# Gate products of a recurrent unit, from whole 128-row products to alternating products of the lower and the upper 64 rows

## The chip, the cores and the metric

The kernel runs on one core of a Trainium2 chip. The metric is the device time of one execution in microseconds (us); lower is better. The engines are TensorE (PE, its weight loads PEld), VectorE (DVE), ScalarE (ACT), GpSimd (POOL) and SyncE (SP), which issues most DMAs.

## What is computed

Two blocks run one after the other on a sequence of 1024 tokens of width 1024. The second block holds a real-gated linear recurrent unit, which is where the change lies. Its gates are products within 16 groups of 64 channels, cut from the reference:

```python
def rg_lru(u, w_rg, b_rg, w_ig, b_ig, lru_lambda):
    ub = uf.reshape(B, S, LRU_BLOCKS, LRU_BLOCK_DIM)          # 16 groups of 64 channels
    r = jax.nn.sigmoid(jnp.einsum('bshi,hij->bshj', ub, w_rg).reshape(B, S, LRU_WIDTH) + b_rg)
    i = jax.nn.sigmoid(jnp.einsum('bshi,hij->bshj', ub, w_ig).reshape(B, S, LRU_WIDTH) + b_ig)
    log_a = -LRU_C * r * jax.nn.softplus(-lru_lambda)
    a = jnp.exp(log_a)
    xin = jnp.sqrt(-jnp.expm1(2.0 * log_a)) * (i * uf)
    # h_t = a_t * h_{t-1} + xin_t, an associative scan over the sequence
```

Ahead of it, u = h @ w_in (a part of it) goes through a causal convolution of 4 taps; behind it, h is multiplied by silu(g_lru) and goes into a product with w_pb.

## The kernel before

All of it is one program with one instruction stream per engine; the order of each stream is written out by hand, and semaphores tie the streams together. Features lie on the 128 partitions, tokens along the free dimension, so a tile c of the recurrent unit holds 128 channels, two groups of 64. PSUM has eight banks of 512 float32 words per partition. The class `Banks` gives the fills (one output of 512 words each) to the banks in turn: fill n takes bank n % 8 and waits (`wait_free`) until fill n - 8 has been drained by the engine that `list_fills_2` names for it.

The weight stream comes in tiles of 128x1024 words. SP loads a tile (`load_tile`) when the last product with the tile before it in its slot is done; POOL then splits it into a high part (L913, a cast) and a low part (L916, a subtraction), and TensorE forms each float32 product in three passes of these parts (`three_passes`, L1017 to L1019). A fill of 8 contraction tiles is 24 such products.

The recurrent unit is worked on in rounds. Round q of 0 to 3 handles c = 2q and 2q+1, and round 4 ends it:

- TensorE fills ("lu", c, h) for both c and both halves h of the tokens (4 fills), then, from round 1 on, ("lg", c-2, h) (4 fills), and then the gate products ("lr", c, h) and ("li", c, h) (8 fills of one float32 product each, L1536, which stands in the trace as two instructions). These use `rgig`, loaded once, as plain float32. Before each c it waits for `uc_ready`, the convolution of that c.
- VectorE (`convolve`) copies a "lu" bank (L2859) and forms the four taps (L2862, L2864, L2866, L2869) for both c. Then `output(c - 2)` multiplies yl by th (L2875) for both c of the round before. Then it forms i*u (L2887) when ("li", c, 1) is drained, and with what ScalarE gives it L2889, L2890, L2893 and the scan L2894. Behind the last round, L2899 forms `yl_lo` from `yl` and `yl_hi`.
- ScalarE drains the "lg" banks with Silu (L2041) and the gate banks with Sigmoid (L2050 into `ra`, L2052 into `ii`). Ahead of a Sigmoid of "lr" it waits, from round 1 on, for `yl_ready`, which counts the outputs: that of tile c - 2. Then Tanh and Exp (L2057, L2058), Sqrt (L2061), with a table load where the function's table changes. Behind the last round, L2065 forms `yl_hi`.

Behind round 4's "lg" fills TensorE fills ("GB", 0, h) and ("GB", 1, h), and then ("B", 0, h), which needs all eight tiles of `yl_lo` (`yl_split`). More GB and B fills and the last product with w_o end the kernel.

Elsewhere, in the first block's state-space mixer, L1203 already forms float32 products of 64 rows and 128 columns, in turn on the lower and the upper 64 partitions and into two banks, with four products of all 128 rows (L1198) between groups of 16 such instructions; only the last of each group's products signals.

In the layout, `rgig` holds for each c a 128x128 matrix for each of the two gates, with the 64x64 weights of the tile's two groups on its diagonal and zeros elsewhere.

Of the kernel before, what the change touches and what calls it, by code (L numbers as in the profile page):

```python
# [9 lines left out]
ACT = mybir.ActivationFunctionType  # L10
AX_X = mybir.AxisListType.X

P = 128
# [4 lines left out]
HALF = 512  # L18
# [317 lines left out]
def build_program(nc, a, out):  # L336
    with ExitStack() as ctx:
# [27 lines left out]
        def at(offset, *dims):  # L365
            placed[0] += 1
            return place(f"buffer{placed[0]}", offset, dims, F32)
# [5 lines left out]
        K = 1024  # L373
# [62 lines left out]
        def col(name, j):  # L436
            return cols[:, COLS[name][0] + j:COLS[name][0] + j + 1]
# [127 lines left out]
        att = at(4 * K, HEADS, SEQ)  # L565
        merged2 = at(32 * K, KD, SEQ)
        mt2 = at(48 * K, 4, HALF)
        rgig = at(48 * K, 8, 2, P)
        uc = at(4 * K, 2, SEQ)
        ra = at(6 * K, 2, SEQ)  # L570
        th = at(12 * K, 2, SEQ)
        ii = at(14 * K, 2, SEQ)
# [43 lines left out]
        drained2 = {"act": sem("act_drained2"), "dve": sem("dve_drained2")}  # L616
# [34 lines left out]
        rgig_loaded = sem("rgig_loaded")  # L651
# [61 lines left out]
        def _(sp):  # L713
# [164 lines left out]
                load_tile(i)  # L878

            sp.wait_ge(merged2_ready, 16)  # L880
            sp.dma_start(rgig.rearrange("p a b c -> p (a b c)"), a["rgig"]).then_inc(rgig_loaded, 16)
            for i in range(I_LRU + 4, I_WO2):
                load_tile(i)
            b2.wait_full(sp, ("GB", 7, 1))
# [119 lines left out]
        def _(pe):  # L1004
            mm, turn = nc.tensor.matmul, nc.tensor.transpose
# [509 lines left out]
            for q in range(5):  # L1515
                if q < 4:
                    for c in (2 * q, 2 * q + 1):
                        w = wait_split_tile(pe, n_tile)
                        n_tile += 1
                        for h in range(2):  # L1520
                            split_feature_tile(b2, ("lu", c, h), w, hT_parts, h, KD)
                if q > 0:
                    for c in (2 * q - 2, 2 * q - 1):
                        w = wait_split_tile(pe, n_tile)
                        n_tile += 1
                        for h in range(2):
                            split_feature_tile(b2, ("lg", c, h), w, hT_parts, h, KD)
                if q == 0:
                    pe.wait_ge(rgig_loaded, 16)
                if q < 4:  # L1530
                    for c in (2 * q, 2 * q + 1):
                        pe.wait_ge(uc_ready, c + 1)
                        for h in range(2):
                            for name, j in (("lr", 0), ("li", 1)):
                                bank = b2.wait_free(pe, (name, c, h))
                                mm(bank[:], rgig[:, c, j, :], uc[:, c % 2, h * HALF:(h + 1) * HALF],  # L1536
                                   start=True, stop=True).then_inc(full2, 1)

            for i, (name, f) in enumerate(B2_TILES):
# [31 lines left out]
        def _(act):  # L1571
# [464 lines left out]
            for q in range(5):  # L2036
                if q > 0:
                    for c in (2 * q - 2, 2 * q - 1):
                        for h in range(2):
                            bank = b2.wait_full(act, ("lg", c, h))  # L2040
                            fn(yl[:, c, h * HALF:(h + 1) * HALF], bank[:], ACT.Silu).then_inc(drained2["act"], 1)  # L2041
                if q == 4:
                    break
                for c in (2 * q, 2 * q + 1):
                    for h in range(2):
                        hs = slice(h * HALF, (h + 1) * HALF)
                        bank = b2.wait_full(act, ("lr", c, h))
                        if q:
                            act.wait_ge(yl_ready, c - 1)
                        fn(ra[:, c % 2, hs], bank[:], ACT.Sigmoid, bias=col("b_rg", c)).then_inc(drained2["act"], 1)  # L2050
                        bank = b2.wait_full(act, ("li", c, h))
                        fn(ii[:, c % 2, hs], bank[:], ACT.Sigmoid, bias=col("b_ig", c)).then_inc(drained2["act"], 1)  # L2052
                for c in (2 * q, 2 * q + 1):
                    b2.wait_drained(act, ("li", c, 1))
                    if c == 0:
                        act.wait_ge(lru_s_ready, 2)
                    fn(th[:, c % 2, :], ra[:, c % 2, :], ACT.Tanh, scale=lru_ns[:, c:c + 1])  # L2057
                    fn(ra[:, c % 2, :], ra[:, c % 2, :], ACT.Exp, scale=lru_s[:, c:c + 1]).then_inc(act_to_lru, 1)  # L2058
                for c in (2 * q, 2 * q + 1):
                    act.wait_ge(lru_to_act, c + 1)  # L2060
                    fn(th[:, c % 2, :], th[:, c % 2, :], ACT.Sqrt).then_inc(act_to_lru, 1)  # L2061
# [876 lines left out]
def _layouts(inputs):  # L2938
# [3 lines left out]
    c = {}  # L2942
# [68 lines left out]
    c["bsB"] = np.ascontiguousarray(bs.transpose(1, 2, 0, 3).reshape(128, 512))  # L3011
    c["wglu"] = np.ascontiguousarray(f["s5_w_glu"][0].reshape(2, 128, 256).transpose(1, 0, 2).reshape(128, 512))
    c["wr"] = np.ascontiguousarray(f["w_router"][0].reshape(8, 128, 16).transpose(1, 0, 2).reshape(128, 128))
    rg = np.zeros((128, 8, 2, 128), np.float32)
    for j, w in enumerate((f["w_rg_2"][0], f["w_ig_2"][0])):
        for i in range(16):
            s = 64 * (i % 2)
            rg[s:s + 64, i // 2, j, s:s + 64] = w[i]
    c["rgig"] = rg.reshape(128, 2048)
    for k in ("w_gate", "w_up", "w_down"):  # L3020
        c[k] = np.ascontiguousarray(f[k][0])
    return c
# [15 lines left out]
```

## Time and profile before

| | |
|---|---|
| median of 3 runs | 2842.61 us (2842.43 to 2844.53) |
| span of the profiled execution | 2842.6 us |
| TensorE products, busy | 2794.4 us, 98% |
| TensorE weight loads, busy | 2291.8 us, 81% |
| VectorE, busy | 1724.6 us, 61% |
| ScalarE, busy | 1308.0 us, 46% |
| GpSimd, busy | 735.0 us, 26% |

The times are of whole executions; the span is from the first to the last instruction of one execution that was profiled, and no other time is given for that execution. A busy time is the union of an engine's instructions; TensorE's products overlap each other in it, since a product is in the pipeline longer than the next one waits to start. The recurrent unit's rounds lie between about 2372 and 2576 us of the span.

### The profile page before, as it was taken

How to read it: one execution, taken by the hardware profiler on the slowest of the kernel's cores; microseconds unless marked ns; L12 is line 12 of the kernel's file. 1: busy time of each engine (PE TensorE's matmuls, PEld its weight loads, DVE VectorE, ACT ScalarE, POOL GpSimd, SP SyncE). 2: the span in 40 equal slices, each digit the busy share in tenths (PEclk: the TensorE clock that was granted, in tenths of full speed). 3: DMA queues.
4: the chain of work that ended last, by engine and by line, in shares of the span. 5: the costliest groups of instructions: out<-in, count | busy, mean ns of one | idle time of the engine just before them, and what ended most of it. 6: DMA issues, size and time to landing. Idle time of an engine off the chain costs nothing.

```text
span 2842.6 us, 34799 instructions
## 1 busy us (share of the span) xinstructions
PE 2794.4 (98%) x13206; PEld 2291.8 (81%) x13206; DVE 1724.6 (61%) x1880; ACT 1308.0 (46%) x1542; POOL 735.0 (26%) x284
## 2 busy tenths in 40 slices
PE   7999999999999999999999999999999999999999
PEld 6887888478888888888888877888988887778887
DVE  8962114888888888888888884131312614864133
ACT  5131013477777777777777763130312312242021
POOL 0012231002222233333332222313222223433330
PEclk9999999999999999999999999999999999999999
DMA  5021114699999999999999953111111411111131
GB/s 165 30 68 37 38 62 155 246 395 388 383 382 383 383 383 383 381 383 381 383 382 381 377 229 112 52 50 55 49 56 56 139 45 67 42 41 45 52 126 59
DMA packets 127074, 555.96 MB, mean 196 GB/s; under 512 B 14545, under 2 KB 22753, under 8 KB 93825
## 3 DMA queue, kind: packets, MB, share of 16 engines
q1 hardware_dynamic: 116160, 523.91, 48.6%
q0 software_dynamic: 5328, 20.07, 2.5%
q10 hardware_dynamic: 5490, 10.62, 1.0%
q8 instruction: 70, 1.15, 0.2%
q14 instruction: 26, 0.21, 0.0%
HBM read 521.42 MB, written 32.09 MB: 195 GB/s over the span
## 4 chain that ended last, share of the span: by engine, by line
PE 90%; DVE 7%; ACT 2%; issue 1%; DMA 0%; ACTq 0%; POOL 0%; SPq 0%; DVEq 0%
PE bank L1351 23%; PE bank L1017 19%; PE bank L1019 19%; PE bank L1018 19%; PE bank L1364 2%; PE bank L1484 1%; PE bank L1455 1%; PE bank L1536 1%; PE bank L1477 1%; ACT buffer L1973 1%; PE bank L1414 0%; PE bank L1373 0%; DVE heT_lo L2628 0%; DVE buffer L2306 0%; ACT heT_hi L1896 0%
## 5 line engine op out<-in xcount | busy, mean ns | idle before, releaser
L2578 DVE TENSOR_TENSOR slots_lo<-buffer,slots_hi 128x2048 fp32r<-128x2048 f32 x383 | 849.2, 2284 | 103.9 <-ACT slots_hi L1850 103.9
L1850 ACT ACTIVATE slots_hi<-buffer 128x2048 fp32r<-128x2048 f32 x384 | 709.1, 1950 | 44.3 <-PE bank L1351 27.5
L1017 PE MATMUL bank<-hT_hi,ring_hi 128*128 128x512 f32 x1216 | 483.9, 398 | 5.2 <-DVE hT_lo L2694 2.2
L1019 PE MATMUL bank<-hT_hi,ring_lo 128*128 128x512 f32 x1216 | 474.0, 390 | 0.0
L1018 PE MATMUL bank<-hT_lo,ring_hi 128*128 128x512 f32 x1216 | 473.6, 389 | 0.0
L976 POOL DMA_INDIRECT xacc<-buffer x15 | 276.6, 18439 | 619.9 <-ACT buffer L1918 619.9
L913 POOL CAST ring_hi<-buffer 128x1024 fp32r<-128x1024 f32 x101 | 114.7, 1136 | 835.9 <-DMA buffer<-in_wstream 806.6
L916 POOL TENSOR_TENSOR ring_lo<-buffer,ring_hi 128x1024 fp32r<-128x1024 f32 x111 | 285.2, 2572 | 51.2 <-ACT ring_hi L1584 43.1
L1017 PEld LDWEIGHTS bank<-hT_hi,ring_hi 128*128 128x128 f32 x1216 | 228.4, 188 | 57.2 <-DVE hT_lo L2694 7.1
L1019 PEld LDWEIGHTS bank<-hT_hi,ring_lo 128*128 128x128 f32 x1216 | 228.2, 188 | 48.2
L1018 PEld LDWEIGHTS bank<-hT_lo,ring_hi 128*128 128x128 f32 x1216 | 228.5, 188 | 46.4 <-issue 1.2
L1351 PE MATMUL bank<-slots_hi,xsT_hi 128*128 128x512 f32 x960 | 257.8, 390 | 4.0 <-DVE xsT_lo L2596 4.0
L1351 PE MATMUL bank<-slots_lo,xsT_hi 128*128 128x512 f32 x960 | 257.4, 390 | 0.0
L1351 PE MATMUL bank<-slots_hi,xsT_lo 128*128 128x512 f32 x960 | 257.4, 390 | 0.0
L1351 PEld LDWEIGHTS bank<-slots_hi,xsT_hi 128*128 128x128 f32 x960 | 180.9, 189 | 41.8 <-issue 4.2
L1351 PEld LDWEIGHTS bank<-slots_lo,xsT_hi 128*128 128x128 f32 x960 | 180.8, 188 | 37.7
L1351 PEld LDWEIGHTS bank<-slots_hi,xsT_lo 128*128 128x128 f32 x960 | 180.8, 188 | 37.7
L1017 PE MATMUL bank<-slots_hi,heT_hi 128*128 128x512 f32 x512 | 202.5, 395 | 3.1 <-DVE heT_lo L2628 3.1
L1019 PE MATMUL bank<-slots_hi,heT_lo 128*128 128x512 f32 x512 | 199.5, 390 | 0.0
L1018 PE MATMUL bank<-slots_lo,heT_hi 128*128 128x512 f32 x512 | 199.4, 389 | 0.0
L1017 PEld LDWEIGHTS bank<-slots_hi,heT_hi 128*128 128x128 f32 x512 | 96.0, 188 | 29.6 <-issue 6.5
L1019 PEld LDWEIGHTS bank<-slots_hi,heT_lo 128*128 128x128 f32 x512 | 96.1, 188 | 20.5
(508 smaller groups left out, 3957.0 us busy)
## 6 DMA issues: line engine op xcount, KB each, us to landing
buffer<-in_w_gate SPq DMA_DIRECT2D x128, 1024.0 KB, 7.6
buffer<-in_w_up SPq DMA_DIRECT2D x128, 1024.0 KB, 4.9
buffer<-in_w_down SPq DMA_DIRECT2D x128, 1024.0 KB, 8.1
buffer<-in_wstream SPq DMA_DIRECT2D x154, 512.0 KB, 3.5
buffer<-in_x SPq DMA_DIRECT2D x16, 512.0 KB, 8.4
od<-buffer ACTq DMA_DIRECT2D x24, 260.0 KB, 2.1
xacc<-buffer SPq DMA_DIRECT2D x8, 512.0 KB, 2.8
h2d<-buffer SPq DMA_DIRECT2D x8, 512.0 KB, 4.9
```

Source lines behind the costliest of these rows:

```text
L913: nc.gpsimd.tensor_copy(high_tile(i), raw).then_inc(tile_high_ready, 1)
L916: nc.gpsimd.tensor_tensor(low_tile(i), raw, high_tile(i).bitcast(F32), ALU.subtract).then_inc(tile_split, 1)
L976: nc.gpsimd.indirect_dma_start(out=xacc, out_offset=bass.IndirectOffsetOnAxis(ap=idx_scatter, axis=0), in_=ys, in_offset=None, compute_op= ...
L1017: mm(bank, lhs[0], rhs[0], start=first, stop=False)
L1018: mm(bank, lhs[0], rhs[1], start=False, stop=False)
L1019: return mm(bank, lhs[1], rhs[0], start=False, stop=last)
L1351: last = mm(psum[first_bank + c][:], x[:, k, :], w_[:, c * HALF:(c + 1) * HALF], start=(k == 0 and x is xsT_hi and w_ is w[0]), stop=(k == ...
L1364: last = mm(psum[4 + c][:], x[:, KD - 1, :], w_[:, c * HALF:(c + 1) * HALF], start=False, stop=x is xsT_lo)
L1455: last = mm(bank[:, i, :], Qh[:, h, tt * P:(tt + 1) * P], Kh[g][:, h, (tt - nw + 1) * P:(tt + 1) * P], start=True, stop=True)
L1477: last = turn(bank[:, h * P:(h + 1) * P], SM[tt % 2][:, h, (nw - 1 - w_) * P:(nw - w_) * P], ident)
L1850: fn(slots_hi[:, n_ % NH, :], slots[n_ % NS], ACT.Copy).then_inc(slot_high_ready, 1)
L2578: tt2(slots_lo[:, place_of(n_), :], slots[n_ % NS], slots_hi[:, n_ % NH, :].bitcast(F32), ALU.subtract).then_inc(slot_split, 1)
```

## The change

`rgig` holds half as much: for each c, rows 0 to 63 are the weights of the lower group, r gate and i gate side by side (64 + 64 columns), and rows 64 to 127 those of the upper group, i gate and r gate. Each gate product now contracts 64 rows: "lr" those of partitions 0 to 63, "li" those of 64 to 127. A bank so holds both gates of one group: in "lr" the lower half of the partitions is r and the upper half is i, both of the lower group; in "li" the lower half is i and the upper half is r, both of the upper group. ScalarE therefore drains each bank with two Sigmoids of 64x512, the second of which marks it as drained, and two of the four for each c and h read one half of the partitions and write the other.

```diff
--- before.py
+++ after.py
@@ -565,7 +565,7 @@
         att = at(4 * K, HEADS, SEQ)
         merged2 = at(32 * K, KD, SEQ)
         mt2 = at(48 * K, 4, HALF)
-        rgig = at(48 * K, 8, 2, P)
+        rgig = at(48 * K, 8, P)
         uc = at(4 * K, 2, SEQ)
         ra = at(6 * K, 2, SEQ)
         th = at(12 * K, 2, SEQ)
@@ -878,7 +878,7 @@
                 load_tile(i)
 
             sp.wait_ge(merged2_ready, 16)
-            sp.dma_start(rgig.rearrange("p a b c -> p (a b c)"), a["rgig"]).then_inc(rgig_loaded, 16)
+            sp.dma_start(rgig.rearrange("p a b -> p (a b)"), a["rgig"]).then_inc(rgig_loaded, 16)
             for i in range(I_LRU + 4, I_WO2):
                 load_tile(i)
             b2.wait_full(sp, ("GB", 7, 1))
@@ -1531,9 +1531,9 @@
                     for c in (2 * q, 2 * q + 1):
                         pe.wait_ge(uc_ready, c + 1)
                         for h in range(2):
-                            for name, j in (("lr", 0), ("li", 1)):
+                            for name, s in (("lr", 0), ("li", 64)):
                                 bank = b2.wait_free(pe, (name, c, h))
-                                mm(bank[:], rgig[:, c, j, :], uc[:, c % 2, h * HALF:(h + 1) * HALF],
+                                mm(bank[:], rgig[s:s + 64, c, :], uc[s:s + 64, c % 2, h * HALF:(h + 1) * HALF],
                                    start=True, stop=True).then_inc(full2, 1)
 
             for i, (name, f) in enumerate(B2_TILES):
@@ -2047,9 +2047,14 @@
                         bank = b2.wait_full(act, ("lr", c, h))
                         if q:
                             act.wait_ge(yl_ready, c - 1)
-                        fn(ra[:, c % 2, hs], bank[:], ACT.Sigmoid, bias=col("b_rg", c)).then_inc(drained2["act"], 1)
+                        low, high = slice(0, 64), slice(64, P)
+                        fn(ra[low, c % 2, hs], bank[low, :], ACT.Sigmoid, bias=col("b_rg", c)[low])
+                        fn(ii[low, c % 2, hs], bank[high, :], ACT.Sigmoid, bias=col("b_ig", c)[low]).then_inc(
+                            drained2["act"], 1)
                         bank = b2.wait_full(act, ("li", c, h))
-                        fn(ii[:, c % 2, hs], bank[:], ACT.Sigmoid, bias=col("b_ig", c)).then_inc(drained2["act"], 1)
+                        fn(ii[high, c % 2, hs], bank[low, :], ACT.Sigmoid, bias=col("b_ig", c)[high])
+                        fn(ra[high, c % 2, hs], bank[high, :], ACT.Sigmoid, bias=col("b_rg", c)[high]).then_inc(
+                            drained2["act"], 1)
                 for c in (2 * q, 2 * q + 1):
                     b2.wait_drained(act, ("li", c, 1))
                     if c == 0:
@@ -3011,12 +3016,9 @@
     c["bsB"] = np.ascontiguousarray(bs.transpose(1, 2, 0, 3).reshape(128, 512))
     c["wglu"] = np.ascontiguousarray(f["s5_w_glu"][0].reshape(2, 128, 256).transpose(1, 0, 2).reshape(128, 512))
     c["wr"] = np.ascontiguousarray(f["w_router"][0].reshape(8, 128, 16).transpose(1, 0, 2).reshape(128, 128))
-    rg = np.zeros((128, 8, 2, 128), np.float32)
-    for j, w in enumerate((f["w_rg_2"][0], f["w_ig_2"][0])):
-        for i in range(16):
-            s = 64 * (i % 2)
-            rg[s:s + 64, i // 2, j, s:s + 64] = w[i]
-    c["rgig"] = rg.reshape(128, 2048)
+    pairs = np.concatenate([f["w_rg_2"][0], f["w_ig_2"][0]], axis=2).reshape(8, 2, 64, 128)
+    pairs[:, 1] = np.concatenate([f["w_ig_2"][0], f["w_rg_2"][0]], axis=2).reshape(8, 2, 64, 128)[:, 1]
+    c["rgig"] = np.ascontiguousarray(pairs.transpose(1, 2, 0, 3).reshape(128, 1024))
     for k in ("w_gate", "w_up", "w_down"):
         c[k] = np.ascontiguousarray(f[k][0])
     return c
```

## Rows read from the trace of the kernel before

**Rows 1.** The page: busy time, share of the span and instructions of each engine.
```profile
PE 2794.4 (98%) x13206; PEld 2291.8 (81%) x13206; DVE 1724.6 (61%) x1880; ACT 1308.0 (46%) x1542; POOL 735.0 (26%) x284
```

**Rows 2.** Chain that ended last, 2300 to 2640: start us, us, what.
```profile
2398.47 3.70 PE bank L1536 x8
...
2445.71 6.87 PE bank L1536 x16
...
2546.51 6.87 PE bank L1536 x16
2553.38 0.23 PE bank L1017
```

**Rows 3.** Waits of PE, 2394 to the end: us in total, times, longest.
```profile
PE bank L1536 <- DVE buffer L2869: 0.4, 1, 0.4
```

**Rows 4.** Timeline of PE, 186 to 200.5: start us, us, instruction.
```profile
187.91 0.71 PE L1198 MATMUL bank<-buffer 128*128 128x128 f32 x4
188.56 1.16 PE L1203 MATMUL bank<-buffer 64*128 64x128 f32 x16
189.65 0.71 PE L1198 MATMUL bank<-buffer 128*128 128x128 f32 x4
```

**Rows 5.** Timeline of ACT, 2385 to 2510 (round 1).
```profile
2447.66 0.69 ACT L2050 ACTIVATE buffer<-bank,buffer 128x512 f32<-128x512 f32 x1
...
2449.38 0.70 ACT L2052 ACTIVATE buffer<-bank,buffer 128x512 f32<-128x512 f32 x1
...
2453.20 1.14 ACT L2057 ACTIVATE buffer<-buffer 128x1024 f32<-128x1024 f32 x1
```

**Rows 6.** Groups of ACT by form: busy us, mean ns | idle before.
```profile
L2041 ACT ACTIVATE buffer<-bank 128x512 f32<-128x512 f32 x16 | 9.5, 598 | 94.0 <-PE bank L1019 94.0
...
L1693 ACT ACTIVATE buffer<-bank 16x512 f32<-16x512 f32 x4 | 2.1, 574 | 1.0 <-PE bank L1166 1.0
```

**Rows 7.** Timeline of DVE, 2385 to 2510.
```profile
2490.55 3.31 DVE L2875 TENSOR_TENSOR buffer<-buffer 128x1024 f32<-128x1024 f32 x1
```

**Rows 8.** Single lines of DVE, 2402 to 2560: minimum/median/maximum ns, first and last start.
```profile
L2862 DVE TENSOR_SCALAR buffer<-buffer x12: 547/548/1589, 2421.3 to 2537.4; 128x512 f32<-128x512 f32 x12
L2864 DVE SCALAR_TENSOR_TENSOR buffer<-buffer x24: 750/752/1527, 2422.9 to 2538.7; 128x512 f32<-128x512 f32 x24
L2869 DVE SCALAR_TENSOR_TENSOR buffer<-buffer x6: 1408/2088/2773, 2429.1 to 2539.5; 128x512 f32<-128x512 f32 x6
L2875 DVE TENSOR_TENSOR buffer<-buffer x6: 1225/2263/3305, 2440.3 to 2547.2; 128x1024 f32<-128x1024 f32 x6
L2894 DVE TENSOR_TENSOR_SCAN buffer<-buffer x6: 2291/2650/3008, 2413.8 to 2518.2; 128x1024 f32<-128x1024 f32 x6
```

**Rows 9.** Timeline of POOL, 2385 to 2600: one tile.
```profile
2477.75 1.08 POOL L913 CAST ring_hi<-buffer 128x1024 fp32r<-128x1024 f32 x1 [4.76 <-DMA buffer<-in_wstream]
2478.91 2.72 POOL L916 TENSOR_TENSOR ring_lo<-buffer,ring_hi 128x1024 fp32r<-128x1024 f32 x1
```

**Rows 10.** Timeline of all engines, 2392 to 2402 (round 0).
```profile
2394.51 3.59 PE L1536 MATMUL bank<-buffer 128*128 128x512 f32 x8
...
2395.57 0.69 ACT L2050 ACTIVATE buffer<-bank,buffer 128x512 f32<-128x512 f32 x1 [49.22 <-PE bank L1536]
```

**Rows 11.** Timelines of ACT and DVE from 2540, and the line of yl_lo.
```profile
2554.00 1.14 ACT L2057 ACTIVATE buffer<-buffer 128x1024 f32<-128x1024 f32 x1
...
2575.82 1.23 DVE L2875 TENSOR_TENSOR buffer<-buffer 128x1024 f32<-128x1024 f32 x1 [0.94 <-ACT buffer L2041]
2578.17 12.23 DVE L2899 TENSOR_TENSOR yl_lo<-buffer,yl_hi 128x1024 fp32r<-128x1024 f32 x8 [1.13 <-ACT yl_hi L2065]
...
L1018 PE MATMUL bank<-yl_lo,ring_hi x18: 389/389/389, 2597.0 to 2619.4; 128*128 128x512 f32 x18
```

**Rows 12.** The page: DMA issues, KB each, us to landing.
```profile
buffer<-in_wstream SPq DMA_DIRECT2D x154, 512.0 KB, 3.5
```

**Rows 13.** Waits of PE; busy by stretch (PE, PEld, DVE, ACT, POOL), clock, DMA.
```profile
PE bank L1351 <- DVE xsT_lo L2596: 4.0, 1, 4.0
...
578.00:584.00 6.00, 6.00 (x18) 4.76 (x17) 4.79 (x6) 4.52 (x4) 0.54 (x1) 0.60 0.92 355
```

## The prediction

> **What bounds the kernel now.** The page comes first: TensorE is busy 98% of the span, and the chain that ended last runs through it here, so what shortens TensorE's own work shortens the kernel, as long as nothing else is late [rows 1]. Next, the chain in order of time in the stretch that the diff touches. I count from the first gate product (2394.51 us = 0 [rows 10]) and call "gates" the products of L1536 of one round q: they start at 0, 51.2, 101.6 and 152.0; the later ones take 6.87 us for 16 instructions (each of the 8 products of a round is two), 0.429 each, and the last round's end at 158.87 (2553.38) [rows 2]. So a round is 50.4 us on TensorE: 6.87 of gates and 43.5 of "lu" and "lg" products. TensorE waits for nothing from here to the end but 0.4 us in round 0 [rows 3]: the stretch is TensorE's, and the reader should ask how close behind the other two engines are. The answer is in the timelines of ScalarE and VectorE [rows 5, 7].
>
> **TensorE's part.** Each gate product was 128x128 by 128x512, half of its weights zeros; now it is 64x128 by 64x512, in the same number. A 64-row product alone is no shorter: it streams the same 512 columns. The gain can only come from a "lr" product (rows 0 to 63) and a "li" product (rows 64 to 127) running at once. The trace has this pattern at L1203: 16 such instructions, two and two on alternate row halves, 128 columns wide, take 1.09 us (188.56 to 189.65) [rows 4]. A quarter of the columns is a quarter of 0.429, 0.107 each, so 16 in a row would take 1.72; 1.09 is half of that and 0.23 more. The four full ones ahead, between two such groups, take 0.65 instead of 4 x 0.107 = 0.43 [rows 4], 0.22 for the change of form. For one round: 6.87/2 = 3.43, +0.23, +0.22, +0.16 because the half without a partner is four times as long here: 4.0 us. That is 2.87 less per round in rounds 1 to 3. In round 0 the second half waits for the convolution of c=1: its products started at 3.96 after a 0.36 wait [rows 2, 3], and VectorE isn't earlier; they now end at 3.96+2.3 = 6.2 instead of 51.2-43.5 = 7.7, 1.4 less. Were TensorE all that mattered, the sum would be 3 x 2.87 + 1.4 = 10.0 us.
>
> **ScalarE's part.** Four Sigmoids of 128x512 for each c become eight of 64x512, 16 for a round instead of 8. Back to back they start every 0.573 us (the first at 2447.66, the fourth at 2449.38) [rows 5]. No half-height one is in the trace; the nearest are 16x512 from a bank, 574 ns, against 598 for 128x512 [rows 6], so I give half the height the full price (bounds: half of it, 0.29, if height did count, which these two rows exclude, and 0.69, its own duration, if they don't overlap). A round's Sigmoids take 16 x 0.573 = 9.17 instead of 5.54 (2447.66 to 2453.20, the last ones at TensorE's pace [rows 5]): Tanh and all behind it come 3.6 us later after the first Sigmoid.
>
> **Who waits for that.** First Sigmoid of round q, then L2057 and the Exp, Sqrt and scans, then the convolutions of round q+1, then output(2q) at L2875, and for that the first Sigmoid of q+1 waits (on yl_ready, L2050): a loop through ScalarE and VectorE. From L2057 to the end of output is 2493.86-2453.20 = 40.7 [rows 5, 7] (the end is 2490.55+3.31). Before, the loop was 5.54+40.7 = 46.2 in a round of 50.4; now it is 9.17+40.7+0.05 = **49.9**, while TensorE's round would be 4.0+43.5 = 47.5. The loop becomes the longer one. It holds TensorE by the banks: the first "lu" (or, at the end, "lg") product behind the gates takes the bank of ("lr",2q,0), eight fills back, which is free after two Sigmoids, 0.573+0.69 = 1.27 after the first.
>
> The 40.7 holds waits of VectorE for GpSimd, which prepares three weight tiles in it. In each round one instruction of each of these kinds is stretched, the longest against the shortest of its kind: L2862 1.59 against 0.55, L2864 1.53 against 0.75, L2875 3.31 against 1.23, L2894 3.01 against 2.29, and both L2869, 2.77 and 1.41, where the same form at L2864 takes 0.75 [rows 8]: 1.0+0.8+2.1+0.7+2.0+0.7 = 7.3. The loop is 42.6 with none. L2869's 2.77 lies at 2479.4, beside L916's 2.72 from 2478.91 [rows 9]; a tile holds VectorE up for at most about 1.05 (L913) and 2.4 (L916 without its own waiting), 3.45, and three tiles paid in full make 53.0. The Trainium skill ("SBUF — State Buffer", Who interferes with whom) has it that of two such operations the second to issue fully blocks until the first finishes. The stretches agree; by this rule with nothing harmless between, the sum would go by the 53.0. After the change the tiles come about 2.9 us earlier and VectorE's work 3.6 later, so the first tile falls among L2889 to L2894, ops with no free gap between, and the last leaves L2875 for the convolution. I take 0.6 more than now: **50.5**.
>
> **The sum.** Round 1's gates start at 51.2-1.4 = 49.8, first Sigmoid 1.95 later as now (2447.66 against 2445.71, a table load lies between [rows 2, 5]): 51.75; the loop from round 0 (first Sigmoid 1.06 [rows 10], +9.17+40.7 = 50.9) isn't late yet. Round 2: gates at 97.3, but the first Sigmoid at 51.75+50.5 = 102.25 instead of 99.25, and TensorE goes on at 103.5, not 101.3, a wait of 2.2. Round 3: gates at 147.0, first Sigmoid 152.75, "lg" from 154.0 after a wait of 3.0; before 158.87. Then B(0) needs all of yl_lo. From the first Sigmoid of round 3: 9.17, then 23.05 from L2057 (2554.00) to the end of the last output (2577.05), then 13.35 until L2899 is done (2590.40) [rows 11]: 152.75+45.6 = 198.3. TensorE comes there 43.6 after 154.0, at 197.6; before, it came at 202.5 (2597.0) [rows 11]. Everything behind hangs on TensorE and moves with it: 202.5-198.3 = **4.2 us** less. The smaller DMA of rgig, and the bias and weight layouts, cost nothing: the load, now 512 KB, lies behind "lu" products, and TensorE doesn't wait for it even at 1024 KB [rows 3]; not covered, it would be one landing of such a size, 3.5 us, once [rows 12]. The profiled span is 2842.6, the median 2842.61, so the sum is made against the same number: 2838.4.
>
> **Rivals.**
> *TensorE stays the bound* (the loop under 48.0): all 10.0 us come, 2832.6. For it: the loop without stretches is 42.6. Against: three tiles a round will still be prepared, and at the measured stretches it is 49.9. The Trainium skill ("TensorEngine Tiling (Array Packing)", Theoretical Speedup) gives up to 2x for a contraction of 64 rows; by that alone half of the some 27.4 us of gates, 13.7, would come, 2828.9. The rows of L1203 show 1.72/1.09 = 1.6x, edges included [rows 4].
> *No overlap*: the increments on every second instruction or the bank waits between them, which L1203 does not have, keep the halves apart. Then 6.87 stays, the edges add 0.4 a round, the loop (50.5) hides under 50.8: 2844.2.
> *The clock*: TensorE's new waits of 2 to 3 us. After an idle 3.97 us the granted clock was 0.60 (partly the lower level, 1.2 GHz) over the next 6 us, 18 products instead of 26, some 2 to 3 us lost [rows 13]. Round 2's loss is covered by the loop; round 3's isn't: TensorE reaches B(0) at 200.6, 2840.7.
> *Slower*: a half-height Sigmoid whose input and output lie 64 partitions apart costs more. Each 0.01 us is paid 16 times in three loops and the tail, 0.64 us. At 0.65 each the gain is gone; at 0.74 the kernel is 0.2% slower; at 0.80 it is 9 to 10 us slower, 2852. Against: the price doesn't show in 16x512 [rows 6].
>
> **How the numbers follow.** The forecast (loop binds, 48 to 52 long) 0.62, with 0.22 of it at 49.7 or less, where it gives over 5.7 us; TensorE bound 0.11; no overlap 0.13; clock 0.08; slower 0.06. A measurement can tell about 0.2%, 5.7 us. Faster 0.22+0.11 = 0.33; same 0.40+0.13+0.08 = 0.61; slower 0.06. Likeliest time 2838.4. The range reaches from nearly all of TensorE's gain (2832.6) past no overlap (2844.2), 2833.0 to 2844.8. The loop with all three tiles in full gives 54.1+2 x 53.0+45.6 = 205.7, 3.2 more than 202.5, 2845.8; that all of them fall so is not likely, and it stays outside.
>
> **What will show it.** 16 gate instructions in about 4 us; half-height Sigmoids every 0.573; the first Sigmoid of rounds 2 and 3 some 50.5 after the one before, released by L2875 and not by TensorE; TensorE waiting 2 to 3 us behind the gates of rounds 2 and 3 for a Sigmoid; little or no wait at B(0). Gates of 6.9 us prove me wrong about the overlap; rounds of 47.5 without waits, about the loop.

## The result, and the profile after

| | before | changed |
|---|---|---|
| median | 2843.34 us (4 runs) | 2858.4 us (2856.79 to 2861.96, 4 runs) |
| ratio to before | | 1.0052, 95% interval 1.0040 to 1.0064 |
| span of the profiled execution | 2842.6 | 2857.3 |

The change makes the kernel 15 us slower. The prediction said 4.2 us faster, with a range up to 2844.8. The profile after, in the order of the prediction. (In the changed kernel ScalarE's Sigmoids are L2051, L2052, L2055 and L2056; lines of VectorE's part are 5 further on: L2892 is i*u, L2894 and L2895 follow, L2899 is the scan, L2869 and L2874 are taps, L2880 is the output, L2904 forms yl_lo.)

TensorE's part, from its timeline (start us, us, instruction), beside [rows 2, 10]; the last row is the first product of B(0):

```profile
2392.77 1.99 PE L1536 MATMUL bank<-buffer 64*128 64x512 f32 x8
...
2500.97 3.79 PE L1536 MATMUL bank<-buffer 64*128 64x512 f32 x8 [4.43 <-DVE buffer L2874]
...
2561.56 0.77 PE L1017 MATMUL bank<-hT_hi,ring_hi 128*128 128x512 f32 x1 [0.32 <-ACT buffer L2052]
...
2609.67 0.47 PE L1017 MATMUL bank<-yl_hi,ring_hi 128*128 128x512 f32 x1 [3.55 <-issue]
```

Eight gate instructions take 1.99 us with the pipeline's end, where eight took 3.59 in [rows 10]: the two row halves do run at once. But TensorE now waits: 4.43 us in rounds 2 and 3 for the second convolution, and 3.55 us ahead of B(0). The profile names no releaser there ("issue"); the kernel has TensorE wait for all of yl_lo ahead of B(0) (`yl_split`), and L2904, which forms it, ends at 2609.56. Its waits in the stretch (us in total, times, longest) were 0.4 in all in [rows 3]:

```profile
PE bank L1536 <- DVE buffer L2874: 11.0, 4, 4.4
PE bank L1017 <- issue: 3.5, 1, 3.5
PE bank L1017 <- ACT buffer L2052: 2.7, 3, 2.1
PE bank L1536 <- DVE buffer L2864: 2.1, 2, 1.1
```

ScalarE, the first Sigmoid of round 1 and then round 2, beside [rows 5]:

```profile
2447.13 0.68 ACT L2051 ACTIVATE buffer<-bank,buffer 64x512 f32<-64x512 f32 x1
...
2502.25 1.28 ACT L2051 ACT_TABLE_LOAD   x1 [9.15 <-DVE buffer L2880]
2503.54 0.68 ACT L2051 ACTIVATE buffer<-bank,buffer 64x512 f32<-64x512 f32 x1
2504.24 0.69 ACT L2052 ACTIVATE buffer<-bank,buffer 64x512 f32<-64x512 f32 x1
2504.95 0.68 ACT L2055 ACTIVATE buffer<-bank,buffer 64x512 f32<-64x512 f32 x1
...
2514.78 1.15 ACT L2062 ACTIVATE buffer<-buffer 128x1024 f32<-128x1024 f32 x1
```

Three things stand here. The round's first Sigmoid comes 56.4 us after that of round 1 (2447.13 to 2503.54), released by the output (L2880): the loop sets the pace, as forecast, but it is 56.4 long and not 50.5. The Sigmoids start every 0.70 us, 16 in 11.24 (2503.54 to 2514.78), not every 0.573. And the table load stands behind the wait for the output, 1.3 us inside the loop.

VectorE and GpSimd in the same turn of the loop (timelines), beside [rows 8, 9]. Each cast shown begins a weight tile, and its subtraction (L916, shown for the first tile) follows it:

```profile
2463.34 1.95 DVE L2895 SCALAR_TENSOR_TENSOR buffer<-buffer 128x1024 f32<-128x1024 f32 x1
2465.20 3.43 DVE L2892 TENSOR_TENSOR buffer<-buffer 128x1024 f32<-128x1024 f32 x1
...
2474.65 1.88 DVE L2898 TENSOR_TENSOR buffer<-buffer 128x1024 f32<-128x1024 f32 x1
2476.57 4.37 DVE L2899 TENSOR_TENSOR_SCAN buffer<-buffer 128x1024 f32<-128x1024 f32 x1
...
2486.29 3.55 DVE L2869 SCALAR_TENSOR_TENSOR buffer<-buffer 128x512 f32<-128x512 f32 x2
...
2495.97 4.15 DVE L2869 SCALAR_TENSOR_TENSOR buffer<-buffer 128x512 f32<-128x512 f32 x2
```

```profile
2463.05 1.16 POOL L913 CAST ring_hi<-buffer 128x1024 fp32r<-128x1024 f32 x1 [12.80 <-DMA buffer<-in_wstream]
2464.28 3.27 POOL L916 TENSOR_TENSOR ring_lo<-buffer,ring_hi 128x1024 fp32r<-128x1024 f32 x1
...
2474.04 1.41 POOL L913 CAST ring_hi<-buffer 128x1024 fp32r<-128x1024 f32 x1 [6.49 <-DMA buffer<-in_wstream]
...
2484.85 1.04 POOL L913 CAST ring_hi<-buffer 128x1024 fp32r<-128x1024 f32 x1 [6.07 <-DMA buffer<-in_wstream]
...
2495.77 1.06 POOL L913 CAST ring_hi<-buffer 128x1024 fp32r<-128x1024 f32 x1 [7.27 <-DMA buffer<-in_wstream]
```

Four tiles meet VectorE's dense work now, not three. By "stretch" I mean the time of an instruction beyond what it takes undisturbed. Against 1.23, 1.22, 1.22, 2.29 and twice 2 x 0.77 (the last two rows are two instructions each), the stretches are 0.7+2.2+0.7+2.1+2.0+2.6 = 10.3, against 7.3 before.

The loop adds up: 42.6 without stretches, +10.3, +2.07 for 16 Sigmoids at 0.70, +1.3 for the table load = 56.3; measured 56.4. Here 42.6 is the prediction's loop without stretches.

The start of B(0) in the kernel before, for comparison:

```profile
2596.75 0.39 PE L1017 MATMUL bank<-yl_hi,ring_hi 128*128 128x512 f32 x1
```

And the clock (from:to in us, the stretch's length, TensorE's busy time and products in it, granted clock, DMA share, GB/s; the last row is an earlier stretch, round 3):

```profile
2606.00:2612.00 6.00, 2.45 (x9) 0.92 0.26 89
2612.00:2618.00 6.00, 6.00 (x23) 0.80 0.00 0
2618.00:2624.00 6.00, 6.00 (x28) 1.00 0.09 23
2556.00:2562.00 6.00, 4.22 (x9) 0.50 0.00 0
```

After the wait of 3.55 us TensorE runs in part at the lower of its levels (1.2 of 2.4 GHz): 23 products in 6 us, where the next 6 us at full clock have 28. B(0) starts 12.9 us later than before (2609.67 against 2596.75), and the kernel's end comes 14.7 later. Of the 1.8 us between, 1.7 are lost in B(0)'s first 18 products, which take 5.78 us instead of 4.08 (2609.67 to 2615.45, before 2596.75 to 2600.83); behind them the two executions keep the same pace. The row of round 3 has a clock of 0.50 around its 4.43 us wait, and the eight gate instructions behind such a wait take 3.79 us instead of 1.99.

### The profile page after: what moved, and what is told of

The parts are those of the page before. It is cut to its first block, busy times and chain, and to the rows that moved or that the text cites. A ratio compares the mean times of both kernels' runs of the same rounds, so it can differ in the third digit from the quotient of the medians.

```text
span 2857.3 us, 34831 instructions
## 1 busy us (share of the span) xinstructions
PE 2789.8 (98%) x13206; PEld 2287.4 (80%) x13206; DVE 1733.5 (61%) x1880; ACT 1330.6 (47%) x1574; POOL 732.8 (26%) x284
## 4 chain that ended last, share of the span: by engine, by line
PE 84%; DVE 10%; ACT 3%; issue 1%; DMA 1%; POOL 0%; ACTq 0%; SPq 0%; DVEq 0%
PE bank L1351 23%; PE bank L1017 18%; PE bank L1019 18%; PE bank L1018 18%; PE bank L1364 2%; PE bank L1484 1%; DVE buffer L2869 1%; PE bank L1455 1%; DVE buffer L2899 1%; PE bank L1477 1%; ACT buffer L1973 1%; PE bank L1414 0%; PE bank L1373 0%; DVE heT_lo L2633 0%; DVE buffer L2898 0%
## 5 line engine op out<-in xcount | busy, mean ns | idle before, releaser
L913 POOL CAST ring_hi<-buffer 128x1024 fp32r<-128x1024 f32 x101 | 114.2, 1130 | 854.2 <-DMA buffer<-in_wstream 854.2
L916 POOL TENSOR_TENSOR ring_lo<-buffer,ring_hi 128x1024 fp32r<-128x1024 f32 x111 | 281.4, 2538 | 51.2 <-ACT ring_hi L1584 43.1
L1677 ACT ACTIVATE buffer<-bank,buffer 128x512 f32<-128x512 f32 x32 | 22.1, 690 | 195.2 <-PE bank L1019 195.2
```

The costliest lines, as they stand in the source:

```text
L913: nc.gpsimd.tensor_copy(high_tile(i), raw).then_inc(tile_high_ready, 1)
L916: nc.gpsimd.tensor_tensor(low_tile(i), raw, high_tile(i).bitcast(F32), ALU.subtract).then_inc(tile_split, 1)
```

## The experiments

All ratios are to the kernel before, run on the same chip (its medians there 2844.2 to 2844.5). The changed kernel itself (2858.4) ran beside a median of 2843.3, so a difference between runs of different groups can be off by about 1 us. First the four that take the change apart.

**The products alone.** The 64-row products of the change, with the drains of before:

```diff
-                        fn(ra[low, c % 2, hs], bank[low, :], ACT.Sigmoid, bias=col("b_rg", c)[low])
-                        fn(ii[low, c % 2, hs], bank[high, :], ACT.Sigmoid, bias=col("b_ig", c)[low]).then_inc(...)
+                        fn(ra[:, c % 2, hs], bank[:], ACT.Sigmoid, bias=col("b_rg", c)).then_inc(...)
... (the same for the "li" bank)
```

> Only the products of the change: 64-row gate products as in the changed kernel, but each bank drained by one Sigmoid of 128x512 as before, so that one half of ra and of ii holds the other gate (the output is not the reference's). Theory A (the loss is the loop through ScalarE and VectorE, not TensorE): the loop is 8 x 0.573 = 4.6 us of Sigmoids, a table load of 1.3 behind the wait if the output is late, and 41 to 44 from L2057 to the end of output, 47 to 49.9 in all against TensorE's 47.5; the kernel gains 4 to 10 us against the one before, about 2836. Rival B (the halves don't pay on TensorE, or its waits and the lower clock cost the time): gates of 4 us but lasting waits, no gain, or slower than before by 5 or more.

Measured: 2833.97 us, ratio 0.9964 (0.9950 to 0.9978), 10.5 us faster. TensorE in this run, from the chain that ended last (start us, us, instructions):

```profile
2399.71 1.99 PE bank L1536 x8
2445.44 3.63 PE bank L1536 x16
2492.86 3.63 PE bank L1536 x16
```

and, from the list of its waits over the stretch, the one (us in total, times, longest):

```profile
PE bank L1536 <- DVE buffer L2869: 1.9, 1, 1.9
```

The rounds are 47.42 us (2445.44 to 2492.86) with no wait behind round 0. TensorE's share of the change is worth what the prediction's sum gave it, 10.0 us, and the loss is not there. Its Sigmoids of full height start every 0.57 us.

**ScalarE's part alone.** The products of before, each bank drained by two half-height Sigmoids, nothing crossing:

```diff
-                        fn(ra[:, c % 2, hs], bank[:], ACT.Sigmoid, bias=col("b_rg", c)).then_inc(...)
+                        fn(ra[low, c % 2, hs], bank[low, :], ACT.Sigmoid, bias=col("b_rg", c)[low])
+                        fn(ra[high, c % 2, hs], bank[high, :], ACT.Sigmoid, bias=col("b_rg", c)[high]).then_inc(...)
... (the same for the "li" bank and `ii`)
```

> Only ScalarE's part of the change: the products of before (128 rows), each bank drained by two Sigmoids of 64x512, lower half to lower half and upper to upper, nothing crosses; the output is the reference's. If the 0.70 us from start to start comes from the half height or from changing halves: 0.70 here too, the loop 11.2+1.3+41 to 44 = 53.5 to 56.5, longer than TensorE's 50.4, so 8 to 17 us slower than before. If it comes from the crossing of partitions: 0.573, the loop 49.9, hidden, within 2 us of before.

Measured: 2859.8 us, 1.0057 (1.0040 to 1.0074); the Sigmoids start 0.70 us apart, and the table load waits for the output here too:

```profile
2504.58 1.28 ACT L2051 ACT_TABLE_LOAD   x1 [8.09 <-DVE buffer L2880]
```

The whole loss comes with ScalarE's part. With it, the faster products give nothing back (2859.8 with the old ones, 2858.4 with the new): the loop hides them.

**Is it the crossing?** The changed kernel with every Sigmoid writing the partitions that it reads (bank low to `ra[low]`, bank high to `ra[high]`, and so for `ii`):

> The changed kernel, but with every half-height Sigmoid writing the partitions that it reads (the gates land in the wrong tiles, the output is not the reference's). If crossing costs the 0.13 us: spacing 0.573, loop 2.1 shorter, about 6 us faster than the changed kernel. If not: 0.70 and 2858, as the changed kernel.

Measured: 2858.91, 1.0054 (1.0037 to 1.0071), spacing 0.70 (2501.36 to 2502.05 to 2502.76). Crossing costs nothing that shows.

This run shows one thing more. Its profiled execution was the fastest of its four, 2853.91 us, and its loop was 52.5 us long in rounds 1 and 2 (the first of these two turns starts at 2448.88):

```profile
2501.36 0.68 ACT L2051 ACTIVATE buffer<-bank,buffer 64x512 f32<-64x512 f32 x1
...
2553.89 0.68 ACT L2051 ACTIVATE buffer<-bank,buffer 64x512 f32<-64x512 f32 x1
```

The Sigmoids and the table load in it take what they take in the changed kernel. VectorE's stretches in a turn add up to 6.3 to 6.4 us instead of 10.3: the weight tiles fall at other places of its chain. So GpSimd's part of the loop is no fixed price; it depends on where the tiles fall.

**Where the wait stands.** The output is waited for because Tanh overwrites `th`; `ra` and `ii` are free earlier, since the gate products themselves come behind the convolution, and that behind the scans.

```diff
                         bank = b2.wait_full(act, ("lr", c, h))
-                        if q:
-                            act.wait_ge(yl_ready, c - 1)
...
+                    if q:
+                        act.wait_ge(yl_ready, c - 1)
                     fn(th[:, c % 2, :], ra[:, c % 2, :], ACT.Tanh, scale=lru_ns[:, c:c + 1])
```

> The changed kernel with the wait for the output of tile c-2 moved from the first Sigmoid to Tanh, the first to overwrite th. Theory A: the table load comes early again (1.3 less) and the first eight Sigmoids (5.6) and the output (1.3 to 2.5) leave the loop, which then runs by the second convolution, the gates and eight Sigmoids: 2.2+5.6+42.6 = about 50.4 instead of 56.5, near TensorE's round of before, 2840 to 2845. If the loop isn't what sets the time, it stays at 2858.

Measured: 2846.94, 1.0008 (0.9998 to 1.0018), 11.5 us less than the changed kernel (a little above what was expected, 2840 to 2845). This cuts the loop where the prediction says that it closes, so the loop is shown as the cause. TensorE's waits left in its profile, one of 4.65 us on the second convolution in round 2 and one at B(0):

```profile
PE bank L1536 <- DVE buffer L2874: 6.8, 3, 4.6
PE bank L1017 <- issue: 4.3, 1, 4.3
```

**The same on the kernel before**, as a control:

> The kernel before with the wait moved to Tanh and nothing else. Its loop (46.2) was hidden under TensorE's 50.4, so theory A expects no change, 2843 to 2845; a gain would mean that the wait cost something in the kernel before too.

Measured: 2843.82, 0.9998 (0.9988 to 1.0007). The wait cost nothing while TensorE set the pace.

**The table load.** The changed kernel, with a Sigmoid of one column ahead of the wait:

```diff
+                        if q and c == 2 * q and h == 0:
+                            fn(root[:, 0:1], root[:, 0:1], ACT.Sigmoid)
                         bank = b2.wait_full(act, ("lr", c, h))
```

> The changed kernel with a Sigmoid of one column ahead of the wait for the output, so that the table is loaded while ScalarE waits. Theory A: 1.3 us minus the 0.2 of the small Sigmoid, hidden too, leave the loop in rounds 1 to 3, in all 3 to 4 us against the changed kernel, 2854 to 2855.5. Rival (the load is hidden elsewhere): no change, 2858.

Measured: 2854.74, 1.0039 (1.0023 to 1.0054), 3.7 us below the changed kernel, as expected, though the two intervals overlap. The profile shows the mechanism: the load ends 7.9 us before the Sigmoid that needs it (2494.69 against 2502.55).

```profile
2493.41 1.28 ACT L2048 ACT_TABLE_LOAD   x1
2494.70 0.20 ACT L2048 ACTIVATE buffer<-buffer 128x1 f32<-128x1 f32 x1
2502.55 0.68 ACT L2053 ACTIVATE buffer<-bank,buffer 64x512 f32<-64x512 f32 x1 [7.64 <-DVE buffer L2882]
```

**Why 0.70 and not 0.573?** Three orders. First, with the wait at Tanh, the four Sigmoids that read the lower half of a bank, then the four that read the upper (the halves written alternate):

```diff
+                        fn(ra[low, c % 2, hs], bank[low, :], ACT.Sigmoid, bias=col("b_rg", c)[low])
+                        fn(ii[high, c % 2, hs], bank[low, :], ACT.Sigmoid, bias=col("b_ig", c)[high])
...
+                        fn(ii[low, c % 2, hs], b2.bank(("lr", c, h))[high, :], ACT.Sigmoid, bias=col("b_ig", c)[low]).then_inc(...)
+                        fn(ra[high, c % 2, hs], b2.bank(("li", c, h))[high, :], ACT.Sigmoid, bias=col("b_rg", c)[high]).then_inc(...)
```

> The kernel with the wait at Tanh (2846.9), with the Sigmoids of a tile c in another order: the four that read the lower half of a bank first, then the four that read the upper half; the output is the reference's. If the 0.70 us come from changing the half that is read from one Sigmoid to the next, six of eight now start after 0.57 and the loop is about 1 us shorter in each round, 2844 to 2846. If they come from the half height itself or the operands, the spacing stays 0.70 and the time too, or rises a little, since the first bank is free two Sigmoids later.

The spacing stayed at 0.69 to 0.71. The time was 2843.86, 0.9998 (0.9989 to 1.0008), 3 us below the run with the wait at Tanh, which the spacing doesn't explain. The intervals overlap, and the cause stays open; its profile has waits of 4.1 us in all on the second convolution and 2.3 at B(0), against 6.8 and 4.3 there. By this run alone I would have blamed half height. Second, the kernel before with half-height Sigmoids, grouped so that four in a row read and write the lower partitions, then four the upper:

> The kernel before with half-height Sigmoids (nothing crosses), for each tile c first the four on the lower 64 partitions, input, output and bias all there, then the four on the upper; the output is the reference's. If a Sigmoid waits for the one before it only where the half changes, six of eight start after 0.57; if half height itself forbids the overlap, all stay at 0.69 to 0.70.

```profile
2450.27 0.68 ACT L2051 ACTIVATE buffer<-bank,buffer 64x512 f32<-64x512 f32 x1
2450.86 0.67 ACT L2053 ACTIVATE buffer<-bank,buffer 64x512 f32<-64x512 f32 x1
2451.43 0.67 ACT L2051 ACTIVATE buffer<-bank,buffer 64x512 f32<-64x512 f32 x1
2452.00 0.68 ACT L2053 ACTIVATE buffer<-bank,buffer 64x512 f32<-64x512 f32 x1
2452.68 0.68 ACT L2056 ACTIVATE buffer<-bank,buffer 64x512 f32<-64x512 f32 x1
2453.27 0.67 ACT L2058 ACTIVATE buffer<-bank,buffer 64x512 f32<-64x512 f32 x1
```

Starts 0.57 apart while the half stays the same, 0.68 where it changes (2452.00 to 2452.68). So half height costs no more than full height. Two successive ones overlap by about 0.1 us if both use the same partitions, and not at all if the next changes the half. A change of the half that is read is enough (in the changed kernel 2503.54 to 2504.24: bank low, then bank high, both writing low), and so is a change of the half that is written, with that of its bias, which changes along (the run before this one); the written half and the bias's were not told apart. The one execution of this run took 2849.72, with loops of 51.7 us in rounds 1 and 2 (56.2 and 52.6 in the profile of ScalarE's part alone, with the same Sigmoids in turn). Third, half heights in turn, without the bias:

> The kernel before with half-height Sigmoids in turn, as in the run with ScalarE's part alone, but without the bias (so the gates lack it, the output is not the reference's). Full-height ones without a bias operand start every 0.49 us (Silu at L2041, two in 1.09), with it every 0.573. If the bias read is what half height makes slower, the spacing falls below 0.6; if half height takes the overlap away whatever the operands, it stays at the length of one, 0.60 to 0.70.

```profile
2448.61 0.59 ACT L2051 ACTIVATE buffer<-bank 64x512 f32<-64x512 f32 x1
2449.21 0.59 ACT L2052 ACTIVATE buffer<-bank 64x512 f32<-64x512 f32 x1
2449.83 0.59 ACT L2055 ACTIVATE buffer<-bank 64x512 f32<-64x512 f32 x1
```

0.61 apart, the length of one (0.59) and a little more: no overlap here either, so the bias is not needed to forbid it. One execution, 2848.11.

**VectorE's order.** With the wait at Tanh, VectorE idles 8 us for the first Exp; i*u of the second tile goes there:

```diff
                 for c in pair:
                     b2.wait_drained(dve, ("li", c, 1))
                     step(tt2(ii[:, c % 2], ii[:, c % 2], uc[:, c % 2], ALU.mult))
+                for c in pair:
                     dve.wait_ge(act_to_lru, 1 + 4 * q + c % 2 + 1)
```

> The kernel with the wait at Tanh (2846.9), and VectorE's i*u of the second tile (L2892) moved ahead of its wait for the first tile's Exp, where VectorE idles 8 us; the output is the reference's. Theory A: 1.25 us, and up to 2.2 more where GpSimd blocked it, leave the loop in each round: the rounds near 48 to 50, 2841 to 2844. If the loop does not set the time: 2846.9.

Measured: 2840.07, 0.9989 (0.9979 to 0.9999): 6.9 us below 2846.94, more than the 3 to 6 expected. TensorE's waits in its profile are shorter at both places than those with the wait at Tanh:

```profile
PE bank L1536 <- DVE buffer L2874: 3.8, 3, 1.9
PE bank L1017 <- issue: 2.2, 1, 2.2
```

So VectorE's chain in the loop is what TensorE waited for.

**GpSimd's hold.** Then three of the four casts (L913) in a round go to ScalarE:

```diff
-HIGH_ON_ACT = FRONT_HIGH + [i for i in SPLIT_TILES if I_WOUT + 2 <= i < I_MOD or i >= I_WO2]
+CASTS = [I_LRU + 6 + 4 * _q + _k for _q in range(3) for _k in range(3)]
+HIGH_ON_ACT = FRONT_HIGH + [i for i in SPLIT_TILES if I_WOUT + 2 <= i < I_MOD or i in CASTS or i >= I_WO2]
```

(with `tile_high` of these tiles, the cast on ScalarE, behind the Sqrts and behind the first and third "lg" Silu of a round)

> The kernel of the run before (i*u moved ahead), and three of the four casts of weight tiles in a round (L913) taken from GpSimd to ScalarE, in ScalarE's idle time between Silus; the subtractions (L916) stay on GpSimd. The output is the reference's. If GpSimd's hold of the port shared with VectorE is what stretches the loop, up to 3 x 1.05 us more leave it in each round: 2836 to 2841, and faster than before. If the stretches have another cause, no change against the run before, or slower, as ScalarE has 3.2 us more work.

Measured: 2838.11, 0.9983 (0.9973 to 0.9993). Faster than before, within what was expected, but the interval overlaps that of the run before it, 2 us above, and TensorE's waits in the profile add up to 6.0 us as they did without it:

```profile
PE bank L1018 <- issue: 3.1, 1, 3.1
PE bank L1537 <- DVE buffer L2879: 2.9, 2, 1.9
```

That the casts' hold is worth anything by itself is not shown.

**The wait at B(0).** It was 3.1 us in that profile, for yl_lo. With the GB products one pair ahead (GB(2) ahead of B(0)):

```diff
-B2_TILES = [("GB", 0)]
+B2_TILES = [("GB", 0), ("GB", 1)]
 for _f in range(8):
-    B2_TILES += ([("GB", _f + 1)] if _f < 7 else []) + [("B", _f)]
+    B2_TILES += ([("GB", _f + 2)] if _f < 6 else []) + [("B", _f)]
```

> The fastest kernel so far (wait at Tanh, i*u early, three casts on ScalarE) with the GB products one pair ahead, so that GB(2) lies ahead of B(0), for which TensorE waited 3.1 us for yl_lo; the output is the reference's. If that wait is worth its length: 2 to 3 us off 2838, about 2835 to 2836, near the 2834 of the products alone. If something else is late there, 2838 as before.

Measured: 2834.96 us, 0.9968 (0.9957 to 0.9979): 9.2 us faster than the kernel before, and 1 us from the products alone. Against the run before it, it is 3.1 us less, the length of the wait, though the two intervals overlap a little. TensorE's waits in the stretch and to the end, with none at B(0):

```profile
PE bank L1535 <- DVE buffer L2877: 2.9, 2, 1.9
```

So nearly all of the change's TensorE gain can be had, once the loop is short enough. The last three rearrangements were not run on the kernel before; as TensorE waits there for 0.4 us in all [rows 3], little is left for them to gain.

## Why the prediction was wrong

The right mechanism was in it, the loop through ScalarE and VectorE. The step that failed is the loop's length, 50.5 us, and in it first of all the price of a half-height Sigmoid, 0.573 us; the wrong sign follows from the sizes.

- *TensorE's part*: 4.0 us of gates forecast, 3.63 measured; 10.0 us in all forecast, 10.5 measured alone. Right, and the rival "no overlap" is out.
- *The loop binds*: right, and shown by moving the wait (11.5 us). Its length was 53.2, 56.4 and 56.5 us from round to round, where the forecast had 50.7 (TensorE's pace), 50.5 and 50.5. The 5.9 us missing in the second are 2.07+1.3+2.4, the next three terms:
- *"Half the height the full price", 0.573*: the largest failure. Measured 0.70, 2.07 us in each turn of the loop and in the tail, 8.3 us of Sigmoids in all. The two rows that I leant on [rows 5, 6] had the same partitions in successive instructions; the upper bound that I named, 0.69, was the right one. The rival "slower" had a price of this kind (break-even at 0.65), with the crossing as the cause; the cause is the change of half. At 0.70 that rival alone would give about 2846.5, so the Sigmoids' price by itself explains about two fifths of the way from 2838.4 to 2858.4.
- *"First Sigmoid 1.95 later as now"*: the table load was counted only there. In the kernel before, the first output was done at 2443.56 (2440.26+3.30), and the load came right behind the last Silu, beside the first gate products:

```profile
2446.36 1.28 ACT L2050 ACT_TABLE_LOAD   x1
```

  Once the output is late, the load stands behind its wait, 1.3 us in each turn. I had left it out of the loop.
- *"0.6 more than now" for GpSimd*: 3.0 more in the changed kernel's profile. Four tiles meet VectorE's dense work there, and it has no gap between the first Exp and the second convolution for any of them. The Trainium skill ("SBUF — State Buffer", Who interferes with whom) says that the second to issue fully blocks until the first finishes; the first tile's rows fit that: L916 ends at 2467.55, and L2892, begun at 2465.20 and 1.22 us long by itself, ends at 2468.63, 1.08 behind it. The stretches are 2.0 to 2.9 us per tile, so 3.45 "in full" is more than any tile took; that four tiles at 2.6 come to the prediction's 53.0 for three in full (42.6+10.3) is chance. The term has no one value either: in the profile without the crossing it was 6.3 to 6.4, 0.9 less than before the change. Even with the forecast's own 7.3+0.6 = 7.9 for it, the other two terms make the loop 53.9, beyond the 48 to 52 of the forecast.
- *Where TensorE is held*: the forecast had it wait for a bank behind the gates, 2 to 3 us in rounds 2 and 3. Only round 1 has such a wait (2.11). In rounds 2 and 3 it waits among the gates, 1.0 us ahead of the last two of the first tile's and 4.43 for the second convolution, and behind them 0.3 for a bank. It is the same loop, caught at another link, and the sum doesn't change by it.
- *The tail*: 45.6 us from the last round's first Sigmoid to yl_lo forecast, 49.5 measured (2560.04 to 2609.56): 2.07 of Sigmoids, and the rest GpSimd again, at L2894 (3.30 us long) and the output.
- *The clock*: a rival at 0.08, real and small. 1.7 us were lost behind the wait at B(0), where the prediction expected little or no wait; in rounds 2 and 3 the loss is hidden by the loop, as the rival said of round 2 alone.
- *A reading*: the 2597.0 that stands in the sum as the start of B(0) is its second product, the first with yl_lo; B(0) begins at 2596.75. That is 0.25 us and changes nothing.

Put together in the prediction's own count: the loops 2.5+5.9+6.0 and the tail 3.9, 18.3 us more, on -4.2: +14.1 at B(0). Measured there from the first gate product, 216.9 against 202.2, +14.7. The clock adds 1.7, and the first gate product came 1.7 earlier in this execution than in the kernel before's: 14.7, the difference of the spans.

The Trainium skill ("TensorEngine Tiling (Array Packing)", PSUM Bottleneck) says that tiling speeds up TensorE but not the copy out of PSUM, which may become the bottleneck; it says so of a fourfold speedup. Here it came at less than twofold, and without a busy ScalarE: it works 47% of the span, yet 11.24 us of drains in place of 5.54, in a loop of waits, cost more than the products won.

## What to carry to other kernels

When work moves onto an engine off the critical path, write down the loop of waits that it stands in, and its whole length, beside the bound engine's period: here a loop of 46.2 us under a period of 50.4 grew by 5.7 (Sigmoids), 1.3 (table load) and 3.0 (GpSimd), which no busy share shows, while the period itself shrank to 47.4. A wait should stand at the first instruction that needs it (here Tanh, not Sigmoid), and a function's table is best loaded ahead of a wait that can be late. A price taken from back-to-back rows holds only for the same order of operands: look at what the row before each of them touches.

## What the runs showed of the hardware that was not expected

- Two successive ScalarE activations overlap by some 0.1 us (0.573 from start to start at 0.69 long) if they use the same partitions. With the half changed, that which is read or that which is written along with its bias, the next starts 0.69 to 0.72 after: no overlap. The Trainium skill ("ScalarE: Activation LUTs", What ACT_TABLE_LOAD costs) has successive activations overlap by about 93 ns, without that condition; the runs agree, at 0.11 us, for the same partitions only. Height 64 (0.68 long) against 128 (0.69) makes no difference.
- A table load stood behind the wait for the output that is ahead of the same Sigmoid (2502.25, right behind L2880). Where that wait was over, it ran right behind the last Silu (2446.36), 0.65 us after the first gate product's start; in round 0 a bank took 1.06 us from there to its Sigmoid [rows 10], so it seems that the load did not wait for the bank.
- Products of alternate row halves with an increment on every second instruction overlap about as well as those of [rows 4], which signal once per group: 16 in 3.63 us, 0.227 each, against 0.429 for whole ones. That is 0.2 us above half of 6.87, and L1203's group was 0.23 above its half.
